# Hybrid encoder step on one core: half A's convolution schedule, the order of high and low products, and the first two FFN tiles of half B reordered

## The chip, the cores and the metric

The kernel runs on 1 core of one Trainium2 chip. Its five engines run their own instruction streams and meet at semaphores: TensorE (PE, matmuls, with weight loads as PEld), VectorE (DVE), ScalarE (ACT), GpSimd (POOL) and SyncE (SP, which issues the DMAs of the weights). The metric is the device time of one execution in microseconds (us), lower is better. It is a median of several runs.

## The reference

A two-layer encoder on 1,024 prompt frames and 32 sample frames, all in float32. Layer 0 is a convolution module and a SwiGLU FFN; layer 1 is windowed attention with 16 query and 4 key heads, and a second FFN.

```
for i in range(DEPTH):
    hp, hs = rms_norm(xp, g_mix[i]), rms_norm(xs, g_mix[i])
    if i % N_MIXERS == 0:
        u = h @ w_pw1 + b_pw1;  g = a * sigmoid(gate)        # 1024 -> 2 x 1024
        c = depthwise causal conv of g, width 31, + b_dw      # per channel
        m = silu(layer_norm(c, ln_g, ln_b)) @ w_pw2 + b_pw2
    else:
        q, k, v = qkv_proj(h, w_qkv, qn_g, kn_g)              # RMS norm per head
        m = sink_attention(q, k, v, dist, valid, sinks) @ w_o
    xp, xs = xp + mp, xs + ms
    x = x + (silu(h @ w_gate) * (h @ w_up)) @ w_down          # h = rms_norm(x, g_ffn[i])
```

The first output is the 1,056 frames after both layers; the others are the last 30 convolution inputs and the newest keys and values.

## The kernel before

**Data.** Channels lie on the 128 partitions, so the width of 1,024 is 8 channel tiles, k = 0 to 7. The frames are cut in half A (512 frames) and half B (544: 512 prompt frames and the 32 sample frames, written as two column groups of 272). The residual `x` stays in SBUF.

**High and low parts.** Each float32 operand is split: a high part (rounded to fp32r) and a low part (the rest). A weight tile of 128 output channels is loaded to `raw`, ScalarE makes `whi` (function `hi`), GpSimd makes `wlo` (`lo`); there are two of each. An activation has `hi_[h]` and `lo_[h]` (`hAh`, `hAl`, `hBh`, `hBl`). One output tile (`proj`) is three groups of products: `whi` times high and low part, alternating over k (L346), then `wlo` times high part (L355). A `mid` hook issues other work between the two. The FFN's down projection (`down`, L560 and L567) does the same with the activations `act`.

**Norms.** A norm is named by its event `ev`: mix0A, mix0B, lnA, ffn0A, lnB, mix1A, ffn0B, mix1B, ffn1A, ffn1B. ScalarE squares 8 tiles, they are summed (for lnA and ffn0A by TensorE itself, `square_sum`, L381, eight matmuls; otherwise by GpSimd, `sum_squares`, L1919), TensorE takes the mean over channels with a matrix of ones (`norm_mean`), ScalarE makes the factor (`factor`: Ln, then Exp), VectorE scales (`x_norm`, L1401), ScalarE rounds the high part (`n_hi_part`, or `ln_part` with Silu for the convolution's norm), VectorE subtracts for the low part (`low`, L1406). The scaled tile lies in one of two buffers `nrm`, so tile k waits for the low part of tile k - 2.

**Order of the work.** All of it is written out by hand, engine by engine. `SEQ1` lists the 29 tiles of the first projection: gate ("g") and value ("a") tiles of half A for channels 0 to 2, then A and B alternating, then three more of B. Within it the convolution of half A runs: of 31 taps per channel tile, `NP["A"]` = 10 are done by ScalarE (product, L987) and GpSimd (sum in `accp`, L1940), and 21 by VectorE in two PSUM banks X and Y (L1508), followed by two joins (X with the GpSimd sum, L1515; then Y, L1520). GpSimd adds the tiles to `csum`; TensorE takes the mean (`("lm", "A")`), VectorE centres, squares follow, the norm lnA, then eight tiles `p2` of the second projection. The convolution of half B runs under the p2 tiles and FFN 0 of half A. Then: p2 of B, QKV of A, FFN 0 of B with the attention of A under it, and so on; the last stretch is FFN 1 of A, then FFN 1 of B (11 groups G, each of four tiles gate/up and, from G = 1 on, the down projection of G - 1).

**PSUM.** Eight banks in two rings of four: `take(key, h, ring)` gives the next bank (two, on an even number, for half B) and waits until its former user has been read. Products use ring 0; small things, and the convolution, ring 1.

**Waits of note.** `act_low` (L1604) makes the low part of the FFN's activations and stands, on VectorE, between the additions `add_to_x` (L1592) of down tiles 3 and 4. In the QKV part of half B, `head_mean` number 2 is issued in the middle of tile 5 and takes two banks of ring 1.

## Time and profile before

| | us |
|---|---|
| median of 3 runs | 2289.23 (2288.8 to 2289.9) |
| profiled execution, its own time | 2286.99 |
| its span, first to last instruction | 2285.2 |
| TensorE busy | 2228.7 |
| VectorE, ScalarE, GpSimd busy | 1111.8, 1037.8, 1113.6 |
| mean granted clock of TensorE | 0.988 of full speed |

The profiled execution's own time is 1.8 us above its span. Engine rows are sums over the span; an engine that is idle costs time only where TensorE waits for it.

### The profile page before, as it was taken

What the parts mean: (1) busy time and instruction counts of PE and PEld (TensorE: products, weight loads), DVE (VectorE), ACT (ScalarE), POOL (GpSimd) and SP (SyncE); (2) the same over time, 40 slices, a digit from 0 to 9 for tenths busy, and PEclk for the clock granted to TensorE, in tenths of its full rate; (3) what the DMA queues carried; (4) which work ended last, traced back from release to release, by engine and by line L of the source; (5) the groups of instructions that cost most, each with busy time, mean ns of one, the idle gap of its engine ahead of it and who ended that gap; (6) DMA issues with size and microseconds to landing.
All of it is one profiled execution on the core that took longest, in us unless ns stands there. A gap on an engine that the chain in (4) does not pass through costs nothing.

```text
span 2285.2 us, 34556 instructions
## 1 busy us (share of the span) xinstructions
PE 2228.7 (98%) x13954; PEld 2017.0 (88%) x13954; DVE 1111.8 (49%) x1822; ACT 1037.8 (45%) x1659; POOL 1113.6 (49%) x573
## 2 busy tenths in 40 slices
PE   8998899999999999999999999999999999999999
PEld 7797678887889799999999898888888989999999
DVE  4987668873434544445443535454554142222223
ACT  6544655533524654544552466465655332222222
POOL 3787569975446533333334544333333443443433
PEclk9999899999999999999999999999999999999999
DMA  4111123332333522222222342222222323233222
GB/s 149 47 54 57 57 65 102 97 102 83 94 100 89 104 86 79 75 74 75 75 75 84 93 99 84 83 83 78 80 84 75 92 77 99 93 102 93 84 89 90
DMA packets 313644, 194.15 MB, mean 85 GB/s; under 512 B 40374, under 2 KB 286734, under 8 KB 313486
## 3 DMA queue, kind: packets, MB, share of 16 engines
q1 hardware_dynamic: 311608, 190.83, 28.3%
q8 instruction: 112, 1.84, 0.3%
q10 hardware_dynamic: 1878, 1.11, 0.2%
q14 instruction: 46, 0.38, 0.1%
HBM read 184.39 MB, written 5.10 MB: 83 GB/s over the span
## 4 chain that ended last, share of the span: by engine, by line
PE 91%; POOL 3%; DVE 2%; ACT 2%; issue 1%; DMA 0%; ACTq 0%; DVEq 0%; POOLq 0%
PE ps L346 42%; PE ps L355 21%; PE ps L560 14%; PE ps L567 7%; PE ps L530 2%; POOL accp L1940 2%; PE ps L516 1%; PE ps L364 1%; PE ps L492 1%; PE ps L491 1%; POOL wlo L1909 1%; PE ps L381 1%; DVE x L1592 1%; POOL rs L1919 0%; DVE sq L1401 0%
## 5 line engine op out<-in xcount | busy, mean ns | idle before, releaser
L1909 POOL TENSOR_TENSOR wlo<-raw,whi 128x1024 fp32r<-128x1024 f32 x342 | 838.9, 2453 | 1095.4 <-PE ps L355 763.7
L857 ACT ACTIVATE whi<-raw 128x1024 fp32r<-128x1024 f32 x342 | 361.8, 1058 | 628.4 <-PE ps L346 366.6
L346 PE MATMUL ps<-hBh,whi 128*128 128x272 f32 x2112 | 440.7, 290 | 6.0 <-DVE x L1592 3.2
L346 PE MATMUL ps<-hBl,whi 128*128 128x272 f32 x2112 | 440.0, 290 | 0.0
L346 PE MATMUL ps<-hAh,whi 128*128 128x512 f32 x1056 | 418.7, 397 | 18.5 <-DVE hAl L1406 10.5
L346 PE MATMUL ps<-hAl,whi 128*128 128x512 f32 x1056 | 416.1, 394 | 0.0
L1592 DVE TENSOR_TENSOR x<-ps,x 128x512 f32<-128x512 f32 (+1 forms) x368 | 258.4, 705 | 244.2 <-PE ps L567 181.3
L346 PEld LDWEIGHTS ps<-hBh,whi 128*128 128x128 f32 x2112 | 334.2, 190 | 8.9 <-issue 4.9
L346 PEld LDWEIGHTS ps<-hBl,whi 128*128 128x128 f32 x2112 | 332.4, 189 | 0.0
L355 PE MATMUL ps<-hBh,wlo 128*128 128x272 f32 x2112 | 291.2, 290 | 0.0
L355 PEld LDWEIGHTS ps<-hBh,wlo 128*128 128x128 f32 x2112 | 273.7, 188 | 2.5 <-issue 1.9
L355 PE MATMUL ps<-hAh,wlo 128*128 128x512 f32 x1056 | 270.6, 399 | 2.9 <-POOL wlo L1909 2.9
L346 PEld LDWEIGHTS ps<-hAh,whi 128*128 128x128 f32 x1056 | 200.3, 190 | 68.8 <-DVE hAl L1406 11.1
L1599 DVE TENSOR_TENSOR s<-ps,s 128x512 f32<-128x512 f32 (+1 forms) x88 | 62.3, 708 | 369.3 <-PE ps L355 367.2
L355 PEld LDWEIGHTS ps<-hAh,wlo 128*128 128x128 f32 x1056 | 197.0, 190 | 46.6 <-issue 4.3
L346 PEld LDWEIGHTS ps<-hAl,whi 128*128 128x128 f32 x1056 | 200.9, 190 | 40.8
L1940 POOL TENSOR_TENSOR accp<-accp,prod 128x512 f32<-128x512 f32 (+1 forms) x144 | 199.7, 1387 | 25.2 <-ACT prod L987 12.4
L1665 DVE TENSOR_TENSOR ptl<-ps,pth 128x512 fp32r<-128x512 f32 (+1 forms) x64 | 42.1, 658 | 167.1 <-ACT pth L1088 167.1
L1508 DVE SCALAR_TENSOR_TENSOR ps<-gxB,dwc,ps 128x574 f32<-128x574 f32 x152 | 114.1, 811 | 0.0
L1088 ACT ACTIVATE pth<-ps 128x512 fp32r<-128x512 f32 (+1 forms) x64 | 36.6, 572 | 167.6 <-PE ps L516 167.6
L1508 DVE SCALAR_TENSOR_TENSOR ps<-gxA,dwc,ps 128x512 f32<-128x512 f32 x152 | 101.8, 749 | 0.0
L560 PE MATMUL ps<-act0h,whi 128*128 128x272 f32 (+1 forms) x288 | 78.6, 327 | 4.5 <-DVE x L1592 3.9
(254 smaller groups left out, 3161.7 us busy)
## 6 DMA issues: line engine op xcount, KB each, us to landing
raw<-in_w_gate_dram SPq DMA_DIRECT2D x88, 512.0 KB, 3.8
raw<-in_w_up_dram SPq DMA_DIRECT2D x88, 512.0 KB, 3.8
raw<-in_w_down_dram SPq DMA_DIRECT2D x88, 512.0 KB, 3.6
raw<-in_w_pw_dram SPq DMA_DIRECT2D x38, 512.0 KB, 4.0
raw<-in_w_qkv_dram SPq DMA_DIRECT2D x32, 256.0 KB, 3.7
raw<-in_w_o_dram SPq DMA_DIRECT2D x64, 128.0 KB, 2.9
stage<-in_x_prompt_dram SPq DMA_DIRECT2D x8, 512.0 KB, 5.7
raw<-in_w_qkv_dram SPq DMA_DIRECT2D x8, 512.0 KB, 3.7
```

The lines of the kernel that those rows point to most:

```text
L346: ins = nc.tensor.matmul(o, whi[n % 2][:, P * k:P * (k + 1)], src[:, k, c0:c0 + w], start=(k == 0 and src is hi_[h]), stop=False)
L355: ins = nc.tensor.matmul(o, wlo[n % 2][:, P * k:P * (k + 1)], hi_[h][:, k, c0:c0 + w], start=False, stop=(k == KD - 1))
L530: ins = nc.tensor.matmul(ps[0:HD, 6, 0:256], v[:, slot, HD * g:HD * (g + 1)], p[:, 256 * z:256 * (z + 1)], start=(z == 0 and w == 0), stop ...
L560: ins = nc.tensor.matmul(o, whi[n % 2][:, wc], src[s + e][:, c0:c0 + w], start=(e == 0 and src is ach), stop=False)
L567: ins = nc.tensor.matmul(o, wlo[n % 2][:, wc], ach[s + e][:, c0:c0 + w], start=False, stop=(e == 1))
L857: nc.scalar.activation(whi[n % 2][:], raw[n % 2][:], ACT.Copy).then_inc(w_hi, 1)
L1508: link(nc.vector.scalar_tensor_tensor((X, Y)[q % 2], two(gx[h][:, c, t:t + w]), dwc[:, KD * t + c:KD * t + c + 1], (X, Y)[q % 2], ALU.mult ...
L1592: nc.vector.tensor_tensor(xd, pt(key), xd, ALU.add).then_inc(fr(key), 1)
L1599: nc.vector.tensor_tensor(s, pt(key), s, ALU.mult).then_inc(fr(key), 1)
L1665: nc.vector.tensor_tensor(ptl[:, 0:w], ps[:, 5, 0:w], f(pth[:, 0:w]), ALU.subtract).then_inc(pt_lo, 1)
L1909: nc.gpsimd.tensor_tensor(wlo[n % 2][:], raw[n % 2][:], f(whi[n % 2][:]), ALU.subtract).then_inc(w_lo, 1)
L1940: nc.gpsimd.tensor_tensor(accp[p % 2][:, 0:w], accp[p % 2][:, 0:w], prod[r % 2][:, 0:w], ALU.add).then_inc(padd, 1)
```

## The change

- The convolution of half A gives ScalarE and GpSimd 9 taps instead of 10, VectorE 22 instead of 21. X and Y alternate between banks 4, 5 and 6, 7, and the two joins of a channel tile stand behind the first six taps of the next. VectorE starts it at once with 8 and 10 steps (before 6 and 6), then 8 per slot (7).
- `SEQ1` loses two tiles of B. Between the mean of the convolution and the p2 tiles now stand one tile ahead of the squares' sum and two behind it; the two value tiles B 1 and B 2 come after p2.
- The squares of lnA are added in pairs by GpSimd (four matmuls instead of eight); those of ffn0A by VectorE (`sum_of_squares`; two matmuls).
- The scaled tiles have eight buffers (`full_`, in the place of the low part) instead of two. The first tile that uses new activations (`new`) does all high products, then `wlo`, then all low ones. `whi` of such a tile is free at its end.
- The first gate and up tiles of the last FFN of half B are done together (`proj_pair`): high products of both, low ones last.
- At the start: 10 and 14 matmuls with no use for their result (`keep_busy`), parameters in another order, the products of tile 0 between the matmuls that scale half A, diagonals of half B by ScalarE, activation tables loaded ahead. The x groups of frames 512 on use a ring of two banks.
- The norm means of mix1A, ffn0B and ffn1A go to ring 1; that of mix1B one tile later, that of ffn1B one half of a down projection earlier. `act_low` stands behind all eight additions. GpSimd's two sums in FFN 0 A, G = 6, stand behind the next `wlo`. In QKV of B the low part of the sample values moves ahead of the head norm of slot 6.

```diff
-NP = {"A": 10, "B": 10}
+NP = {"A": 9, "B": 10}
...
-SEQ1 += [("g", "B", 0), ("a", "B", 0), ("g", "B", 1)]
+SEQ1 += [("g", "B", 0)]
...
+    for p in range(KD):
+        out += own[p][:6] + ends + own[p][6:-2]
+        ends = own[p][-2:]
+    return out + ends
...
-        want = 0 if s < 2 else 1 if s in (5, 6) else 6 if s < 5 else 7
+        want = (0, 0, 8, 10, 10, 2, 2)[s] if s < 7 else 8
...
+def products_a(s):
+
+    return 0 if s < 2 else 2 * s - 1 if s < 7 else 11 + (KD * NP["A"] - 11) * (s - 6) // (len(SEQ1) - 7)
...
+        RINGS = [(0, 4), (4, 4), (6, 2)]
...
+                new = ev and (ev, h) != ("mix0", "A") and waited.get(h, 0) < h_need(ev, KD - 1)
...
+                    ins = product(whi, hi_, k, start=(k == 0))
+                    if not new:
+                        ins = product(whi, lo_, k)
...
+                for k in range(KD):
+                    ins = product(wlo, hi_, k, stop=(not new and k == KD - 1))
+                if new:
+                    for k in range(KD):
+                        wait_h(h, ev, k)
+                        ins = product(whi, lo_, k, stop=(k == KD - 1))
...
+            keep_busy(10)
...
+            keep_busy(14)
+            half_a(0)
+            half_a(1)
...
+                     ahead=(lambda k: half_a(k + 2)) if s == 0 else None)
...
-            pe.wait_ge(csummed, KD - 1)
-            mean(("lm", "A"), "A", ones_d, csum)
-            proj("B", ("a", "B", 1), "mix0", load(("a", 1)))
-            square_mean("lnA", lambda k: pe.wait_ge(sq_ready, k + 1))
+            b = take(("lm", "A"), "A")
+            pe.wait_ge(csummed, KD - 2)
+            nc.tensor.matmul(ps[:, b, :], ones_d[:], csum[:, 0:512], start=True, stop=False)
+            pe.wait_ge(c_ready, KD)
+            nc.tensor.matmul(ps[:, b, :], ones_d[:], gx["A"][:, ORDER["A"][-1], 0:512], start=False, stop=True
+                             ).then_inc(pfull[b], 1)
+            proj("B", ("a", "B", 0), "mix0", load(("a", 0)))
+            take(("mean", "lnA"), "A")
+            square_sum("lnA", range(0, KD, 2), lambda i: pe.wait_ge(sq_pairs, i + 1))
+            for c in (1, 2):
+                proj("B", ("g", "B", c), "mix0", load(("g", c)))
...
-                        norm_mean(ev)
+                        norm_mean(ev, 1)
...
-                if n >= 2:
-                    act.wait_ge(whi_free, n - 1)
+                if n - 2 in whi_read:
+                    act.wait_ge(whi_free, whi_read[n - 2])
+                elif n >= 2:
+                    full(act, last_tile[n - 2])
...
                 for k in range(k0, k1):
                     x_norm(ev, k, gain)
-                    if k % 2:
-                        low(ev[-1], ev[:-1], k - 1)
-                        low(ev[-1], ev[:-1], k)
+                for k in range(k0, k1):
+                    low(ev[-1], ev[:-1], k)
...
+                nc.vector.tensor_tensor(sqx[:, 0, :], sqx[:, 0, :], sqx[:, k, :], ALU.add).then_inc(sq_sums, 1)
...
-                        if d == 3:
+                        if d == (3 if G in (0, NG - 1) else KD - 1):
                             act_low(l, h, G, 1)
...
+            lo()
+            for i in range(KD // 2):
+                pool.wait_ge(sq_ready, 2 * i + 2)
+                nc.gpsimd.tensor_tensor(sqx[:, 2 * i, :], sqx[:, 2 * i, :], sqx[:, 2 * i + 1, :], ALU.add
+                                        ).then_inc(sq_pairs, 1)
+            lo()
             lo()
```

`proj_pair`, new, called for the first two tiles of FFN 1 of half B:

```
for n, out in zip(ns, outs_of):
    pe.wait_ge(w_hi, n + 1)
    for k in range(KD):
        pe.wait_ge(h_hi[h], h_need(ev, k))
        ...                                # whi x high part
    pe.wait_ge(w_lo, n + 1)
    ...                                    # wlo x high part
for key, n, out in zip(keys, ns, outs_of):
    for k in range(KD):
        wait_h(h, ev, k)
        ...                                # whi x low part
```

What stands on VectorE around one join of half A's convolution (gxA is its input and result, dwc the taps, accp the GpSimd sum, dv the semaphore of VectorE's own chain, padd that of GpSimd's additions). Before:

```order
L1508 SCALAR_TENSOR_TENSOR ps<-gxA,dwc,ps 128x512 [waits dv] x12
L1469 SCALAR_TENSOR_TENSOR gxA<-ps,col,s 128x512 [waits pfull3,pfree2]
L1508 SCALAR_TENSOR_TENSOR ps<-gxA,dwc,ps 128x512 [waits dv] x7
L1515 SCALAR_TENSOR_TENSOR accp<-ps,col,accp 128x512 [waits dv,padd]
L1520 TENSOR_TENSOR gxA<-ps,accp 128x512 [waits dv]
L1504 TENSOR_SCALAR ps<-gxA,dwc 128x512 [waits gx_edges,pfree1]
```

And in the change:

```order
L1647 SCALAR_TENSOR_TENSOR ps<-gxA,dwc,ps 128x512 [waits dv] x6
L1643 TENSOR_SCALAR ps<-gxA,dwc 128x512 [waits c_ready,gx_edges,pfree1]
L1643 TENSOR_SCALAR ps<-gxA,dwc 128x512
L1647 SCALAR_TENSOR_TENSOR ps<-gxA,dwc,ps 128x512 [waits dv] x4
L1654 SCALAR_TENSOR_TENSOR accp<-ps,col,accp 128x512 [waits dv,padd]
L1659 TENSOR_TENSOR gxA<-ps,accp 128x512 [waits dv]
```

The wait for GpSimd's sum (padd) moved behind six taps of the next tile.

On TensorE, around the mean of the convolution of half A. Before:

```order
L355 MATMUL ps<-hBh,wlo 128x272 x15
L364 MATMUL ps<-csum,ones_d 128x512 [waits pfree2,csummed]
L346 MATMUL ps<-hBh,whi 128x272 [waits w_hi,pfree0]
...
L381 MATMUL ps<-sqx,ones_d 128x512 [waits sq_ready,pfree2]
L381 MATMUL ps<-sqx,ones_d 128x512 [waits sq_ready] x7
```

And in the change, up to the first p2 tile:

```order
L559 MATMUL ps<-csum,ones_d 128x512 [waits csummed,pfree2]
L561 MATMUL ps<-gxA,ones_d 128x512 [waits c_ready]
L395 MATMUL ps<-hBh,whi 128x272 [waits w_hi,pfree0]
...
L469 MATMUL ps<-sqx,ones_d 128x512 [waits sq_pairs,pfree2]
L469 MATMUL ps<-sqx,ones_d 128x512 [waits sq_pairs] x3
...
L395 MATMUL ps<-hAh,whi 128x512 [waits h_hiA,w_hi,pfree6]
L395 MATMUL ps<-hAh,whi 128x512 [waits h_hiA] x7
L395 MATMUL ps<-hAh,wlo 128x512 [waits w_lo]
L395 MATMUL ps<-hAh,wlo 128x512 x7
L395 MATMUL ps<-hAl,whi 128x512 [waits h_readyA] x8
```

The mean has two tiles of B less ahead of it, the sum of squares is four matmuls, two tiles of B (left out in the second gap) follow it, and the first p2 tile asks for its low parts last.

On TensorE in QKV of half B, from the middle of tile 4 to the middle of tile 5. Before (rs is the sum of squares of the norm ffn1A, tq the squared heads):

```order
L364 MATMUL ps<-rs,ones_d 128x512 [waits pfree0,ssum]
...
L364 MATMUL ps<-tq,ones_h 128x272 [waits pfree7,pfree6,hsq]
```

And on TensorE and then VectorE in the change (the last row but one is the sample values' low part, which frees their bank, 7):

```order
L780 MATMUL ps<-ident,qraw 32x128 [waits pfree6]
L780 MATMUL ps<-ident,qraw 32x128
L456 MATMUL ps<-rs,ones_d 128x512 [waits pfree4,ssum]
...
L456 MATMUL ps<-tq,ones_h 128x272 [waits pfree7,pfree6,hsq]
```

```order
L1539 SCALAR_TENSOR_TENSOR hA<-x,col,rs 128x512 [waits rs_ready]
L1539 SCALAR_TENSOR_TENSOR hA<-x,col,rs 128x512
L1544 TENSOR_TENSOR hAl<-hA,hAh 128x512 [waits h_hiA] x2
L1881 TENSOR_TENSOR vtl<-ps,vth 32x256 [waits kv_hi]
L1841 SCALAR_TENSOR_TENSOR qraw<-qraw,col,tq 128x544 [waits hrs]
```

The mean moved from bank 0 (ring 0) to bank 4 (ring 1); the ring's next pair is therefore 6 and 7, where the second value tile and the sample values lie, and bank 7 is freed only behind the two low parts.

## Rows read from the trace of the kernel before

**Rows 1.** The page, part 1: engine busy time, share of the span, instructions.

```profile
PE 2228.7 (98%) x13954; PEld 2017.0 (88%) x13954; DVE 1111.8 (49%) x1822; ACT 1037.8 (45%) x1659; POOL 1113.6 (49%) x573
```

**Rows 2.** Waits of TensorE: total us, times, longest us.

```profile
PE ps L346 <- DVE hAl L1406: 10.5, 6, 7.1
PE ps L364 <- POOL csum L1962: 8.9, 1, 8.9
PE ps L346 <- ACT s L968: 4.8, 1, 4.8
...
PE ps L346 <- DVE x L1592: 4.0, 2, 3.2
PE ps L560 <- DVE x L1592: 3.9, 3, 1.3
PE ps L346 <- ACT qraw L1143: 3.7, 2, 1.9
...
PE ps L355 <- POOL wlo L1909: 2.9, 1, 2.9
...
PE ps L364 <- POOL rs L1919: 1.1, 1, 1.1
```

**Rows 3.** Windows: length; busy PE, PEld, DVE, ACT, POOL; PEclk, DMA share, GB/s.

```profile
60.40:72.20 11.80, 6.97 (x24) 5.66 (x25) 7.74 (x12) 7.63 (x11) 5.91 (x4) 0.86 0.31 89
...
83.10:193.50 110.40, 110.40 (x725) 102.71 (x724) 99.16 (x157) 56.53 (x79) 97.30 (x70) 1.00 0.16 45
193.50:216.30 22.80, 13.92 (x98) 12.67 (x98) 17.65 (x28) 9.20 (x13) 21.43 (x15) 0.82 0.22 64
216.30:237.30 21.00, 13.89 (x65) 9.74 (x64) 8.05 (x15) 11.94 (x17) 2.46 (x2) 0.91 0.17 51
237.30:288.70 51.40, 50.13 (x194) 37.90 (x195) 39.12 (x57) 33.08 (x45) 36.48 (x22) 0.88 0.22 62
288.70:318.80 30.10, 27.35 (x138) 20.32 (x137) 16.95 (x25) 14.65 (x19) 8.98 (x6) 0.94 0.18 52
...
536.00:550.00 14.00, 11.12 (x44) 8.71 (x43) 3.31 (x6) 6.11 (x9) 11.63 (x7) 0.88 0.26 75
...
1856.30:1880.50 24.20, 20.98 (x102) 18.30 (x101) 18.57 (x25) 12.47 (x16) 7.14 (x3) 0.86 0.21 60
```

**Rows 4.** The chain in order of time: start us, us, what.

```profile
223.32 6.88 PE ps L381 x16
...
1797.15 4.02 PE ps L346 x32
1803.16 4.03 PE ps L346 x32
```

**Rows 5.** Timeline, TensorE, the last third of two half A tiles.

```profile
98.84 1.98 PE L355 MATMUL ps<-hAh,wlo 128*128 128x512 f32 x8
...
104.28 1.98 PE L355 MATMUL ps<-hAh,wlo 128*128 128x512 f32 x8
```

**Rows 6.** Timeline, VectorE, half A convolution: a run of taps, the last join.

```profile
86.64 9.31 DVE L1508 SCALAR_TENSOR_TENSOR ps<-gxA,dwc,ps 128x512 f32<-128x512 f32 x14
...
212.24 0.69 DVE L1520 TENSOR_TENSOR gxA<-ps,accp 128x512 f32<-128x512 f32 x1
```

**Rows 7.** Timeline, ScalarE: a table load and the last high part of the norm.

```profile
230.21 1.28 ACT L881 ACT_TABLE_LOAD   x1 [7.38 <-PE ps L381]
...
245.67 0.63 ACT L906 ACTIVATE hAh<-sq 128x512 fp32r<-128x512 f32 x1
```

**Rows 8.** Timeline, VectorE, `act_low`, beside a GpSimd pass and alone.

```profile
956.50 2.85 DVE L1604 TENSOR_TENSOR act3l<-s,act3h 128x544 fp32r<-128x544 f32 x1
...
1851.54 0.68 DVE L1604 TENSOR_TENSOR act1l<-s,act1h 128x512 fp32r<-128x512 f32 x1
```

**Rows 9.** Timeline, half B QKV, tile 5: ScalarE, then VectorE.

```profile
1353.30 1.06 ACT L857 ACTIVATE whi<-raw 128x1024 fp32r<-128x1024 f32 x1 [3.31 <-PE ps L346]
...
1354.91 1.29 DVE L1406 TENSOR_TENSOR hAl<-sq,hAh 128x512 fp32r<-128x512 f32 x2 [3.37 <-ACT hAh L893]
```

More of the change, by code:

```diff
@@ L971, in _, with taps @@
             done = {"A": 0, "B": 0}
-            def taps(h, j):
-                for i in range(done[h], products(h, j)):
+            def taps(h, n):
+                for i in range(done[h], n):
                     p, c, t, r = in_order(h, i)
```

375 lines of the change are left out of this document (230 added, 145 removed).

## The prediction

> **What bounds the kernel now.** I read the page's first part, then the waits of TensorE, then windows around each long wait. TensorE is busy 98% of the span [rows 1], so a gain can only come from its waits, from stretches at the lower clock, or from matmuls left out. A half B tile starts every 6.03 us [rows 4], a half A tile every 5.44 us [rows 5]; neither changes. The eight kinds of wait in [rows 2] sum to 39.8 us. Most lie before 320 us. There TensorE waits for ScalarE's sigmoid (4.8 us, once), for the last GpSimd sum of half A's convolution (8.9 us, once) and for low parts (10.5 us in six waits). Then the clock: PEclk is a share of 2.4 GHz and is a mean of two levels, so 0.86 over 11.8 us means that 3.3 us ran at 1.2 GHz, which costs 1.65 us. In each window of [rows 3] with a PEclk below 1, TensorE had waited for some us shortly before. By the windows, (1 - PEclk) times length is 1.7, 4.1, 1.9, 6.2, 1.8 and 1.7 us for the first row and the third to the seventh, and 3.4 us for the last.
>
> **The sum, part by part.** Positions are those of the profiled execution, whose own time of 2286.99 us is 2.2 us under the median; I subtract gains from the median.
>
> (a) To 83.1 us: 7. At the start VectorE's diagonals no longer stand behind the copy of parameters, but 14 matmuls and the interleaved scaling do fill TensorE; by the rates of the other matmuls the first tile should end some 3.3 us earlier. The next tile takes the same bank and so waits for a sigmoid, 1 us. Two x groups of five tiles run through two banks instead of four: each may stall 0.9 us, -1.8. Diagonals of half B from ScalarE, +1.3. The wait for a sigmoid (4.8 us [rows 2]) was long because ScalarE stood behind products that GpSimd had not taken; with two products a slot instead of three and the table loaded ahead, only the sigmoid, 1 us, is left: +3.8. The clock stays up: +1.7 [rows 3]. Sum 7.3.
>
> (b) The mean of the convolution: 3. A tap costs VectorE 9.31 / 14 = 0.665 us [rows 6]. From 37.6 us on (my estimate: half A's first value was scaled by 41 us before, less some 3.3) it has 192 steps, 128 us; value products, 10 us; 16 passes for half B's norm, 12 us; waits for sigmoid and factors, 2 us. That is 190. In the norm passes both inputs are in SBUF; [rows 8] shows such a pass at 2.85 us beside a GpSimd pass and 0.68 alone. GpSimd has some 10 us of work in that stretch; I take 4 us of collisions, bounds 0 and 8. The convolution ends at 194 instead of 212.9 [rows 6], the mean at 195. Before it was there at 216.3, but with two more tiles (12.1 us) done. So 216.3 - 195 - 12.1 - 1 (a clock that may fall in a wait of 4 us) = 8.2, of which 7.3 were had in (a): +1 to +5 over the bounds, 2.5 taken. Hidden under this is the join: it may now come 4 us later than its sum without a stall.
>
> (c) From the mean to the first p2 tile: 11.6. Before 237.3 - 216.3 = 21.0 [rows 3]. Now one tile, 6, until the last pair sum 3.5 with four matmuls (6.88 us for eight before [rows 4]) and two tiles, 12.1: 21.6, of which 12.1 are the moved tiles.
>
> (d) Eight p2 tiles: 2.2. Before 51.4 us [rows 3], of which 43.5 are work. The high parts of the norm ended 16.1 us after the mean of squares (230.2 [rows 4] to 246.3 [rows 7]). The two tiles cover 12.1. Two table loads of 1.28 [rows 7] leave the chain (-2.6), two `hi` of 1.06 [rows 9] enter it (+2.1), and, at a guess, one collision of a scaling or low pass (+1.7, bounds 0 and 4.4, two at the 2.2 of [rows 8]): 17.3. TensorE gets the last high part 5.2 us into the p2 tile, which after it still has 3.6 us of products instead of ending at 5.44: a stall of 3.6, and 2 for the clock. 43.5 + 5.7 = 49.2.
>
> (e) To the second FFN tile: 7.6. Before 30.1 us [rows 3]. Two matmuls instead of eight save 5.1. The norm ffn0A takes Ln, Exp, 8 scalings and 8 low parts, some 13.3 us and up to 4.6 of collisions, over 8.1 of cover and 5.2 until the last low part is needed: stall 0 to 4.6, taken 2.3, against some 5 before. VectorE's six extra sums (0.6 us, or 2 us in a collision) may cost 0 to 3, taken 0.5.
>
> (f) `wlo` late at 543 us: 2.9 [rows 2] and 1.7 for the clock [rows 3]: 4.5, since GpSimd's two sums no longer stand ahead of it.
>
> (g) The norm mean in QKV of A: 1.9 of the 3.7 us for qraw [rows 2], and 1.2 for the clock that fell there too: 3.
>
> (h) `act_low` behind the additions: the three waits of L560 (3.9 us [rows 2]) go, and two short ones in FFN 0 of A (1): 4.9. It stalled the additions because it took 2.85 us [rows 8]. Behind them it has over 5 us until `down` needs it.
>
> (i) Means of mix1A and mix1B: 1.1 and 1.9, from L1919 (1.1) and the 0.8 of L1592 [rows 2]: 3.
>
> (j) QKV of B: -3. The mean in ring 1 saves 1.8 us of waiting for qraw. But `head_mean` 2 now takes banks 6 and 7, and 7 is freed by the sample values' low part, which stands on VectorE behind two low parts of the norm; these wait for two high parts, those for a `hi` that waits for the high products of this very tile 5. Read from the trace: the `hi` starts at 1353.30, right after the products, the two low passes end at 1356.2, the pass behind them takes 0.4 [rows 9]. So a new wait of 3.5 us in the middle of tile 5, perhaps with 1.2 for the clock.
>
> (k) FFN 1 of half B: 5. The window 1856.3 to 1880.5 has TensorE idle for 3.2 us (24.20 less 20.98) and 3.4 of clock [rows 3]; part of the low clock fell on the idle time itself, so I take 6.1 for both. Now the mean is taken 5 us earlier and only the fourth bank's addition is missing at the start: 0.8 us. 6.1 - 0.8 = 5.3.
>
> Sum: 7.3 + 2.5 + 11.6 + 2.2 + 7.6 + 4.5 + 3 + 4.9 + 3 - 3 + 5.3 = 48.9, so 2289.2 - 49 = 2240 us.
>
> **A rule against it.** [Rows 8] shows a VectorE pass that starts during a GpSimd pass and ends 0.6 us after it. The Trainium skill (SBUF — State Buffer, Who interferes with whom) says that a VectorE instruction with two SBUF inputs and a GpSimd instruction that reads SBUF exclude each other, and whichever comes second is fully blocked. The trace agrees, and by that rule VectorE's new sums over squares and the earlier norm passes, under a GpSimd that is hardly ever idle, are the worst case; it is the second rival.
>
> **Rivals.**
> 1. The convolution does not end sooner. In 83.1 to 193.5 VectorE is busy 99 of 110 us and GpSimd 97 [rows 3]; VectorE gets a tap more per tile. If it ended at 212.9 as before, the mean would come at 214 and (b) be 216.3 - 214 - 12.1 - 7.3 = -17 instead of 2.5: 2260. Against it: it starts 7 us sooner, and loses the waits at the joins. 8%.
> 2. The passes with two SBUF inputs collide. 54 of them (16 for mix0B, 16 for lnA, 6 sums, 16 for ffn0A) now run beside GpSimd work. Each collision costs up to 2.2 us [rows 8]. Ten more on the path than I count: 2262. 10%.
> 3. Slower. The same mechanism, at the same place, if VectorE lost every race: 54 x 2.2 = 119 us. It decides from 25 more collisions on the path (55 us), 2295. Against it: GpSimd has seven passes or so in each of these stretches, and a pass can be lost to only one of them. 2%.
> 4. All waits before 320 us vanish, since the lower bounds of collisions hold and the clock stays up: (b) +2.5, (d) +5.5, (e) +3: 2229, and without the new wait in (j) 2225. 12%.
> 5. The stalls only move: no change. 1%.
>
> **How the numbers follow.** The forecast has the rest, 67%, and its own range is 2230 to 2254: the bounds of (a) +-3, (b) -2 to +3, (d) and (e) -7 to +4, (g) to (k) +-3, not all at once. To hold 8 in 10 I take half of rivals 1 and 2 and of 4: 2227 to 2258. Within 0.2% (4.6 us) is about what a measurement of this kernel can't tell from no change. Faster 0.97 (forecast and rivals 1, 2, 4), same 0.01, slower 0.02.
>
> **What the profile after would show.** (a) Value tile A 2 starts near 59 us. (b) The last join ends at 190 to 196 us and TensorE's wait for it is about 4 us. (c, d) The p2 tiles start near 217 us with one wait of 3 to 5 us for high parts. (f, h) No wait for `wlo` L1909 and none of the down products for additions. (j) A new wait of 3 to 4 us for VectorE at `head_mean` in QKV of B. (k) At most 1 us ahead of the paired tiles. The forecast is wrong if VectorE ends the convolution after 200 us, or if half B's tiles in that stretch begin to wait for their banks, since the value products stand behind VectorE's steps: then (b) goes first.

## The result and the profile after

| | before | after |
|---|---|---|
| median (runs) | 2289.02 us (4) | 2258.39 us (4: 2257.91 to 2258.83) |
| span of the profiled execution | 2285.2 us | 2257.0 us |
| TensorE busy | 2228.7 us | 2214.2 us |
| mean granted clock | 0.988 | 0.995 |

The ratio is 0.9867, with a 95% interval of 0.985 to 0.9884. The change makes the kernel 30.6 us faster. The forecast was 2240 us, 49 us faster, with a range that ended at 2258, just under the result: about three fifths of the forecast gain came. (One execution of an experiment below, that with GpSimd's part a slot earlier, took 2713 us at a mean clock of 0.752; it is left out of that kernel's median.) The engines' rows of the page ([rows 1] has those of before):

```profile
PE 2214.2 (98%) x13984; PEld 2013.2 (89%) x13984; DVE 1113.2 (49%) x1831; ACT 1035.6 (46%) x1659; POOL 1120.6 (50%) x568
```

TensorE is still busy in 98% of the span. TensorE's waits, as in [rows 2] (total us, times, longest us):

```profile
PE ps L395 <- DVE gxB L1612: 7.5, 1, 7.5
PE ps L561 <- DVE gxA L1659: 6.2, 1, 6.2
PE ps L437 <- ACT hBh L1019: 4.0, 1, 4.0
PE ps L456 <- DVE vtl L1881: 3.5, 1, 3.5
PE ps L395 <- ACT hAh L1030: 2.7, 2, 1.8
...
PE ps L395 <- DVE gxA L1606: 2.2, 1, 2.2
...
PE ps L609 <- DVE col L1770: 1.5, 1, 1.5
```

Of the waits in [rows 2] those for `wlo`, for additions ahead of down products (L560 there) and for the norm sum `rs` are gone. The wait for low parts in six pieces (10.5 us) is gone too, but for one of 0.6 us at the start, and in its place stands one of 7.5 us for the scaling of a value tile of half B (L1612). A new one of 4.0 us is for a high part of the last norm (L437, in `proj_pair`), one of 3.5 us for `vtl` (L1881). The wait for the convolution is 6.2 us instead of 8.9.

Windows of the profile after; the columns are those of [rows 3]:

```profile
191.10:199.40 8.30, 2.13 (x6) 0.78 (x5) 4.97 (x8) 2.99 (x4) 7.23 (x5) 0.73 0.22 64
199.40:222.40 23.00, 23.00 (x155) 20.57 (x154) 13.62 (x22) 17.61 (x25) 9.91 (x6) 0.95 0.17 49
222.40:271.20 48.80, 45.98 (x194) 37.09 (x193) 39.88 (x53) 30.57 (x41) 38.06 (x21) 0.97 0.29 86
271.20:300.70 29.50, 21.63 (x126) 18.77 (x125) 24.40 (x36) 12.24 (x18) 14.33 (x9) 0.88 0.25 72
1839.30:1858.60 19.30, 14.08 (x98) 13.50 (x97) 9.20 (x15) 5.98 (x8) 8.46 (x3) 0.91 0.20 55
```

The second to fourth rows answer to the rows at 216.3, 237.3 and 288.7 of [rows 3], the last one to that at 1856.3. The worst is the fourth: 29.5 us of which TensorE works 21.6, at a mean PEclk of 0.88.

**Where the gain went.** The table compares the start of the same matmuls in the two traces. "Ahead by" is the start before less the start after. At the mean of the convolution the two tiles moved behind it (12.06 us) are taken off. "Step" is the change from the row above.

| point | before | after | ahead by | step | forecast |
|---|---|---|---|---|---|
| `wlo` products of value tile A 2 (a) | 70.43 | 63.97 | 6.5 | +6.5 | +7.3 |
| tile behind the mean of the convolution (b) | 215.24 | 199.41 | 3.8 | -2.7 | +2.5 |
| first p2 tile (c) | 237.30 | 222.37 | 14.9 | +11.2 | +11.6 |
| tile behind the last p2 tile (d) | 288.54 | 271.22 | 17.3 | +2.4 | +2.2 |
| `wlo` products, FFN 0 A, tile 2 (e) | 322.28 | 304.31 | 18.0 | +0.7 | +7.6 |
| `wlo` products, behind the late `wlo` (f) | 550.22 | 527.99 | 22.2 | +4.3 | +4.5 |
| a tile behind the mean of mix1A (i) | 708.83 | 685.45 | 23.4 | +1.2 | +1.1 of 3 |
| QKV A behind the mean (g) | 773.76 | 746.60 | 27.2 | +3.8 | +3 |
| FFN 0 B behind the third `act_low` (h) | 1139.92 | 1108.20 | 31.7 | +4.6 | +4.9 |
| behind the mean of mix1B (i) | 1300.13 | 1266.31 | 33.8 | +2.1 | +1.9 of 3 |
| QKV B and first FFN tiles (j) | 1430.85 | 1402.09 | 28.8 | -5.1 | -3 |
| third tile of the last FFN (k) | 1890.56 | 1862.70 | 27.9 | -0.9 | +5.3 |

(a), (c), (d), (f), (g), (h) and (i) came within 1 us of their forecast. They are read from the two traces alone: no experiment takes one of them out by itself, apart from the order of products and the matmuls at the start. (b), (e), (j) and (k) did not, and together they are 20 of the 21 us that the profiled execution lacks. The experiments go to these four places, and to the order of products that the title of the change names.

### The profile page after: what moved, and what is told of

The parts are those of the page before. It is cut to its first block, busy times and chain, and to the rows that moved or that the text cites. A ratio compares the mean times of both kernels' runs of the same rounds, so it can differ in the third digit from the quotient of the medians.

```text
span 2257.0 us, 34608 instructions
## 1 busy us (share of the span) xinstructions
PE 2214.2 (98%) x13984; PEld 2013.2 (89%) x13984; DVE 1113.2 (49%) x1831; ACT 1035.6 (46%) x1659; POOL 1120.6 (50%) x568
## 4 chain that ended last, share of the span: by engine, by line
PE 90%; DVE 3%; POOL 3%; issue 2%; ACT 1%; DMA 0%; SPq 0%; DVEq 0%; POOLq 0%; ACTq 0%
PE ps L395 60%; PE ps L680 15%; PE ps L687 7%; POOL accp L2089 2%; PE ps L648 2%; PE ps L634 1%; PE ps L456 1%; DVE hB L1539 1%; PE ps L609 1%; PE ps L610 1%; POOL wlo L2058 1%; POOL rs L2068 0%; PE ps L497 0%; DVE hA L1539 0%; DVE hAl L1544 0%
## 5 line engine op out<-in xcount | busy, mean ns | idle before, releaser
L2058 POOL TENSOR_TENSOR wlo<-raw,whi 128x1024 fp32r<-128x1024 f32 x342 | 849.8, 2485 | 1057.0 <-PE ps L395 658.3
L395 PE MATMUL ps<-hBh,whi 128*128 128x272 f32 x2080 | 428.4, 289 | 5.0 <-DVE gxA L1606 2.2
L395 PE MATMUL ps<-hBl,whi 128*128 128x272 f32 x2080 | 427.6, 289 | 0.0
L395 PE MATMUL ps<-hAh,whi 128*128 128x512 f32 x1056 | 411.7, 394 | 12.7 <-DVE gxB L1612 7.5
L395 PE MATMUL ps<-hAl,whi 128*128 128x512 f32 x1056 | 409.1, 392 | 0.0
L395 PEld LDWEIGHTS ps<-hBh,whi 128*128 128x128 f32 x2080 | 325.4, 189 | 8.2 <-issue 3.5
L395 PEld LDWEIGHTS ps<-hBl,whi 128*128 128x128 f32 x2080 | 324.0, 188 | 0.0
L2089 POOL TENSOR_TENSOR accp<-accp,prod 128x574 f32<-128x574 f32 (+1 forms) x136 | 191.6, 1409 | 30.8 <-ACT prod L1111 19.1
L1647 DVE SCALAR_TENSOR_TENSOR ps<-gxA,dwc,ps 128x512 f32<-128x512 f32 x160 | 107.3, 746 | 0.0
```

Source lines behind the costliest of these rows:

```text
L395: ins = nc.tensor.matmul(o, wt[n % 2][:, P * k:P * (k + 1)], src[h][:, k, c0:c0 + w], start=start, stop=stop)
L1647: link(nc.vector.scalar_tensor_tensor((X, Y)[q % 2], two(gx[h][:, c, t:t + w]), dwc[:, KD * t + c:KD * t + c + 1], (X, Y)[q % 2], ALU.mult ...
L2058: nc.gpsimd.tensor_tensor(wlo[n % 2][:], raw[n % 2][:], f(whi[n % 2][:]), ALU.subtract).then_inc(w_lo, 1)
L2089: nc.gpsimd.tensor_tensor(accp[p % 2][:, 0:w], accp[p % 2][:, 0:w], prod[r % 2][:, 0:w], ALU.add).then_inc(padd, 1)
```

## The experiments

Each kernel is the changed kernel with the edit shown, unless the text names another; the kernel before, timed beside them, had medians between 2288.7 and 2289.6 us. I compare medians with the 2258.4 us of the changed kernel. A stretch at the low clock is 3.4, 6.8 or 10.2 us long in the traces of the experiments and costs half of that. Traces of kernels that are the same up to that place differ by one or two of them, so a difference of 2 us needs its local reading in the trace as well. In the diffs "..." and comments stand for code that is left out. Line numbers in an experiment's rows are its own, a few off those of the change.

### (e) The value tiles' reader behind the norm

Timeline of the changed kernel, VectorE and TensorE around the first FFN tile (start us, us, what, idle before and its releaser):

```profile
279.98 7.45 DVE L1539 SCALAR_TENSOR_TENSOR hA<-x,col,rs 128x512 f32<-128x512 f32 x8 [5.04 <-ACT rs L1009]
...
287.36 4.89 DVE L1544 TENSOR_TENSOR hAl<-hA,hAh 128x512 fp32r<-128x512 f32 x8
...
292.18 1.96 DVE L1612 SCALAR_TENSOR_TENSOR gxB<-ps,col,s 128x272 f32<-128x272 f32 x6
...
293.25 2.08 PE L395 MATMUL ps<-hAh,whi 128*128 128x512 f32 x4 [7.51 <-DVE gxB L1612]
```

TensorE ends the value tile B 2 at 285.7 us and then stands until 293.25. It doesn't wait for the norm: it waits for `gxB` (L1612), the scaling that frees the banks of the value tile B 1. The two value tiles fill all four banks of ring 0, and their scaling (the function `glu`) stands behind all 16 passes of the norm ffn0A.

```diff
-            norm_parts("ffn0A", C_FFN[0], 0, KD)
             glu("B", 1)
+            for k in range(KD):
+                x_norm("ffn0A", k, C_FFN[0])
             glu("B", 2)
+            for k in range(KD):
+                low("A", "ffn0", k)
```

> VectorE scales value tile B 1 ahead of the norm ffn0A and value tile B 2 between its eight scalings and its eight low parts; nothing else differs from the changed kernel (2258.4 us). Theory: the first gate tile of FFN 0 waits 7.5 us at 285.7 us only for the bank that value tile B 1 holds, because its reader stands behind 16 norm passes; the wait goes or falls to the 1 to 2 us that the high and low parts need, and the low clock after it (6.8 us at half speed) with it: 6 to 9 us faster, 2249 to 2252. Rival: the norm itself is late, as the forecast had it, and the bank only hides that wait: the tile then waits for high parts for 5 us or more, and the time falls by less than 2 us, 2257.

2253.1 us, 5.3 us faster than the change: the theory, though short of the 6 to 9 us that it expected. Its trace:

```profile
285.11 1.09 PE L395 MATMUL ps<-hAh,whi 128*128 128x512 f32 x4
...
286.53 2.06 PE L395 MATMUL ps<-hAh,whi 128*128 128x512 f32 x4 [0.33 <-ACT hAh L1019]
...
288.00 4.87 POOL L2155 COPY stc<-gxB 128x90 f32<-128x90 f32 x1 [6.20 <-DVE gxB L1612]
...
323.06 0.50 PE L395 MATMUL ps<-hAh,whi 128*128 128x512 f32 x1 [1.59 <-ACT s L1191]
```

The first FFN tile starts at 285.1, straight behind the tile ahead of it, and waits 0.33 us for a high part. Its `wlo` products start 8.4 us sooner than in the changed kernel (296.82 against 288.43). So the bank was the cause; the rival has fallen. At the second tile, the point (e) of the table, this kernel is 7.5 us ahead of the changed one: with the bank free (e) would read +8.2, where the forecast had +7.6. At 355 us 5.2 of the 8.4 are left, and at 389 us 4.3: at 323.06 TensorE waits 1.6 us for a sigmoid that stands on ScalarE behind products that GpSimd has not taken. I put that down to GpSimd's copy at 288.00: GpSimd stood idle for 6.2 us ahead of it, and it took 4.87 us beside VectorE's low parts (0.26 us in the changed kernel, where they are done by then).

> The kernel with the value tiles' scaling ahead (2253.1 us), in which GpSimd's copy of half B's first rows (4.87 us there, idle before it for 6.2 us) no longer stands ahead of the first low part and sums of FFN 0 but behind those of its second tile. Theory: of the 8.1 us won at the first FFN tile 3.8 were given back because GpSimd, idle and then blocked at that copy, ran late with its sums, ScalarE behind it with products and a sigmoid (1.6 us of waiting at 321 us, 1.1 at 374); with the copy out of the way they are kept: 2249.5 to 2251. Rival: the tiles of FFN 0 are paced by the convolution of half B as a whole, wherever GpSimd starts: 2253 within 0.8.

```diff
-            freed(pool, ("a", "B", 2))             # and the copy, ahead of FFN 0
+                            if (G, b) == (0, 1):
+                                first_rows()       # the same, behind the sums of tile 2
```

This edit is made in the kernel of 2253.1 us. It takes 2259.0 us, 5.9 slower: both theories missed. Its waits of TensorE:

```profile
PE ps L395 <- ACT hAh L1019: 2.1, 2, 1.7
...
PE ps L395 <- DVE hAl L1544: 1.5, 2, 1.3
```

GpSimd's `wlo` now falls on the norm's passes instead. TensorE waits for a high part (L1019, 1.7 us) and a low part (1.3 us) of ffn0A, and the `wlo` products of the second tile start 4.5 us later. By 380 us all but 1.3 of these 4.5 us have come back. The rest of the 5.9 us goes with the clock: the three unprofiled runs have a mean of 0.993 to 0.994, those of the kernel it starts from 0.996 to 0.997. No trace shows where it fell, since the profiled execution was the fastest of the four (2255.7 us). That the copy caused what was given back stays unproven.

### (b) What ends the convolution

Timeline of the changed kernel: the first join of half A's convolution that has to wait, and the last one, with GpSimd's sums:

```profile
68.29 3.74 POOL L2089 TENSOR_TENSOR accp<-accp,prod 128x512 f32<-128x512 f32 x2 [3.36 <-ACT prod L1111]
...
72.07 0.75 DVE L1654 SCALAR_TENSOR_TENSOR accp<-ps,col,accp 128x512 f32<-128x512 f32 x1 [2.62 <-POOL accp L2089]
...
194.08 2.67 POOL L2089 TENSOR_TENSOR accp<-accp,prod 128x512 f32<-128x512 f32 x2 [0.44 <-POOL accp L2089]
...
196.79 0.75 DVE L1654 SCALAR_TENSOR_TENSOR accp<-ps,col,accp 128x512 f32<-128x512 f32 x1 [2.17 <-POOL accp L2089]
197.57 0.69 DVE L1659 TENSOR_TENSOR gxA<-ps,accp 128x512 f32<-128x512 f32 x1
```

VectorE waits 2.6 us at the first join and 2.2 at the last for GpSimd's sum; the last join ends at 198.26 us. The forecast had 194, and had called this wait hidden. At the last join the sum stands on GpSimd behind a `wlo` (188.34 to 190.76 us). The first is late for another reason: GpSimd had been idle for 3.36 us, waiting for ScalarE's product. That product stood behind four high parts of the norm mix0B, and they waited for scalings, one of which took 2.84 us instead of 0.69 beside a `wlo`. At the six joins between, VectorE does not wait.

The two waits, 4.8 us, are the whole delay. The forecast's other terms, read from VectorE's timeline: the steps start at 39.3 us (37.6 forecast), 192 steps take 127.6 us (128), the value products 10.1 (10), the 16 norm passes 14.0 with their collisions (16), waits for sigmoid and factors 2.3 (2).

```diff
-NP = {"A": 9, "B": 10}
+NP = {"A": 10, "B": 10}
```

> The changed kernel with ten taps of half A's convolution on ScalarE and GpSimd instead of nine, as the kernel before has them; VectorE has 184 steps instead of 192, the slots of the first joins are shifted to fit. Theory that VectorE's steps set the end of the convolution: 8 x 0.665 = 5.3 us sooner, of which the mean gains 4 to 5: 2254. Theory that GpSimd sets it (97.6 us of work in the 115 us before the end, eight more sums of 1.3 us): the end comes 3 to 10 us later: 2262 to 2268. Both bind in turn: 2258.4 within 2.

(The slots of the first joins are shifted to fit.) 2265.9 us, 7.5 slower, inside the range of the second theory. VectorE has 5.3 us less to do, and yet its last join comes 5.0 us later. It waits for GpSimd's sum at five of the eight joins, 11.0 us in all, and longest at the last:

```profile
201.80 0.75 DVE L1654 SCALAR_TENSOR_TENSOR accp<-ps,col,accp 128x512 f32<-128x512 f32 x1 [4.25 <-POOL accp L2089]
```

The same with eight products (every second slot has nine of VectorE's steps instead of eight):

```diff
-NP = {"A": 9, "B": 10}
+NP = {"A": 8, "B": 10}
```

> The changed kernel with eight taps of half A's convolution on ScalarE and GpSimd instead of nine; VectorE has 200 steps instead of 192. With ten taps the mean came 5.0 us later. Theory that GpSimd alone sets the end: 5 us sooner, 2253.5. Theory that both engines bind, and nine is the balance: VectorE's eight more steps cost 5.3 us and save at most the 4.8 us that it waits at the first and the last join: 2258 to 2260, the wait for the last join's GpSimd sum gone. Rival: 2256, if the last slot's wait goes and collisions become fewer.

2263.3 us, 4.9 slower, and outside what any of its theories gave. Only the first join still waits (0.5 us), and yet the last one starts 1.0 us later than in the changed kernel:

```profile
197.78 0.75 DVE L1654 SCALAR_TENSOR_TENSOR accp<-ps,col,accp 128x512 f32<-128x512 f32 x1
```

So with ten products GpSimd sets the end of the convolution, with eight VectorE, and nine is where both bind. The profiled execution with eight is as long as the changed kernel's (2257.1 against 2257.0 us of span) and was the fastest of four; what made the other three 4 us longer no trace shows, beyond a mean clock of 0.993 instead of 0.994. By its trace eight products cost 1.0 us at the join and nothing at the end; that they cost 4.9 us stands on the three other runs. Spreading GpSimd's part so that it ends a slot earlier does not help:

```diff
-    ... 11 + (KD * NP["A"] - 11) * (s - 6) // (len(SEQ1) - 7)
+    n = ... 11 + (KD * NP["A"] - 11) * (s - 6) // (len(SEQ1) - 8)
+    return min(n, (KD - (s < len(SEQ1) - 3)) * NP["A"])
```

> The products and sums of half A's convolution on ScalarE and GpSimd are spread so that they end one slot earlier (68 of 72 are due where 65 were, and all of them one slot ahead of the last). Theory: at the end of the convolution VectorE waits 2.2 us for GpSimd's sum of the last channel tile, which stands behind a low part of a weight tile; without that wait the mean comes 2.2 us sooner: 2256.2. Rival: VectorE, not GpSimd, sets the end, through its 192 steps and its norm passes, and the two more collisions that a fuller GpSimd makes eat the rest: 2258.4 within 0.7.

2259.2 us (2254.3, 2259.2 and 2259.3): near the rival's time, but not for its reason. Its waits at the mean:

```profile
PE ps L560 <- POOL csum L2112: 2.5, 1, 2.5
...
PE ps L562 <- DVE gxA L1660: 1.4, 1, 1.4
```

The join's wait for GpSimd is gone, the join ends 1.5 us sooner, and now the sum over channels (`csum`), also on GpSimd, is late. Of the 1.5 us the tile behind the mean keeps 0.3. The work of GpSimd was only put in another order.

### (k) The pair of the last FFN

Timeline of the changed kernel, VectorE's scalings (L1539) between the additions, GpSimd's `wlo`, and the pair's first product:

```profile
1830.64 2.24 DVE L1539 SCALAR_TENSOR_TENSOR hB<-x,col,rs 128x544 f32<-128x544 f32 x1
...
1837.19 2.40 POOL L2058 TENSOR_TENSOR wlo<-raw,whi 128x1024 fp32r<-128x1024 f32 x1 [4.89 <-ACT whi L981]
...
1837.29 2.88 DVE L1539 SCALAR_TENSOR_TENSOR hB<-x,col,rs 128x544 f32<-128x544 f32 x1
...
1842.79 0.66 ACT L1019 ACTIVATE hBh<-hB 128x544 fp32r<-128x544 f32 x1 [0.64 <-DVE hB L1539]
...
1843.75 2.61 PE L437 MATMUL ps<-hBh,whi 128*128 128x272 f32 x10 [4.04 <-ACT hBh L1019]
```

A scaling alone takes 0.77 us. The second of the eight took 2.24, and the sixth 2.88, beside the `wlo` of 1837.19 (each is a single pass: the expectations below miscount them). The eighth high part is ready at 1843.4 and TensorE, done with the down tiles at 1839.6, waits 4.0 us for it. A low stretch follows (3.4 us from 1843.5 on, 1.7 us lost). Then the third tile waits for the bank of the pair's gate tile, whose sigmoid stands behind a table load:

```profile
1856.59 1.28 ACT L1191 ACT_TABLE_LOAD   x1
...
1858.61 0.49 PE L395 MATMUL ps<-hBh,whi 128*128 128x272 f32 x2 [1.19 <-ACT s L1191]
```

The kernel before has no such wait. There a whole tile of 6 us lies between the end of the gate tile and the next use of its banks; in the pair only the 2.2 us of the other tile's low products do (until 1857.4 us), and `whi`, table and sigmoid take ScalarE until 1858.5. The three terms are 6.9 us, where the forecast had 0.8. No kernel here was built without the pair, so that the third is due to it is read from the rows and not tested.

```diff
+                if n == len(tags) - 1 - tags[::-1].index(("G", 1, 0)):
+                    pool.wait_ge(xn_ready, 7 * KD)
```

> The changed kernel in which GpSimd makes the low part of the first paired weight tile (at 1837.2 us) only after VectorE's last scaling of the norm ffn1B; it is needed 3.6 us after that. Theory: of the 4.0 us that TensorE waits for the last high part, 2.1 are this one collision (2.88 us for two passes and more, 0.77 alone) and 1.5 the one before it (2.24); without the second the wait is 1.9 to 2.2 and the clock stays up or not: 1.9 to 3.6 us faster, 2254.8 to 2256.5. Rival: additions and scalings take turns at the pace of TensorE's own down tiles, and the last high part comes late whatever GpSimd does: 2258.4 within 0.7, the wait still 3.5 or more.

2255.3 us, 3.1 faster. The sixth and eighth scaling, the `wlo`, and the same wait:

```profile
1837.14 0.77 DVE L1539 SCALAR_TENSOR_TENSOR hB<-x,col,rs 128x544 f32<-128x544 f32 x1
...
1839.73 0.77 DVE L1539 SCALAR_TENSOR_TENSOR hB<-x,col,rs 128x544 f32<-128x544 f32 x1
...
1840.67 5.23 POOL L2060 TENSOR_TENSOR wlo<-raw,whi 128x1024 fp32r<-128x1024 f32 x2 [8.51 <-DVE hB L1539]
...
1841.46 2.24 PE L437 MATMUL ps<-hBh,whi 128*128 128x272 f32 x16 [1.89 <-ACT hBh L1019]
```

The wait is 1.9 us, the low clock behind it is gone too, and the pair's `wlo` products start 3.7 us sooner: the theory. One collision, moved away, gives 3 us. The `wlo` could be moved because it was early: it ended at 1839.6 us in the changed kernel, and its first product starts at 1847.3. The other way to give it slack:

```diff
-                    if (l, h) == (1, "A"):
-                        x_norm("ffn1B", d, C_FFN[1])
+                    if (l, h) == (1, "A") and d < 4:
+                        x_norm("ffn1B", 2 * d, C_FFN[1])
+                        x_norm("ffn1B", 2 * d + 1, C_FFN[1])
```

> In the last down projection of FFN 1 of half A VectorE does two scalings of the norm ffn1B ahead of each of the additions 0 to 3 instead of one ahead of each of 0 to 7. Theory: the wait of 4.0 us for the last high part ahead of the paired tiles comes from two scalings that collide with GpSimd's low parts of the weights (2.24 for two and 2.88 for two passes and more, where 0.77 is the price of one alone), at the end of a chain without slack; early scalings have slack, so the wait falls under 1 us and the clock stays up: 3 to 5 us faster, 2253.5 to 2255.5. Rival: the additions come later now, and TensorE waits for their banks what it no longer waits for high parts: 2258 (within 1).

2257.3 us, 1.1 faster, with runs from 2256.9 to 2259.4 us: the rival. The wait for the high part is gone from the list, and TensorE waits for the additions instead, ahead of two down products (and 1.1 us ahead of the pair):

```profile
PE ps L680 <- DVE x L1738: 2.2, 2, 1.9
```

The two collisions (3.62 us for the first two scalings, 3.00 for the last two) are still there and now delay the additions. VectorE is late by what the collisions cost, and the order only chooses who waits.

### (j) The sample values' low part

Timeline of the changed kernel, QKV of half B (the norm's factor is there at 1313.6 us):

```profile
1315.93 1.41 DVE L1539 SCALAR_TENSOR_TENSOR hA<-x,col,rs 128x512 f32<-128x512 f32 x2
...
1319.05 1.29 DVE L1544 TENSOR_TENSOR hAl<-hA,hAh 128x512 fp32r<-128x512 f32 x2 [1.71 <-ACT hAh L1019]
1320.26 0.41 DVE L1881 TENSOR_TENSOR vtl<-ps,vth 32x256 fp32r<-32x256 f32 x1
...
1320.81 1.73 PE L456 MATMUL ps<-tq,ones_h 128*128 128x272 f32 x4 [3.47 <-DVE vtl L1881]
```

The chain is the one that the forecast had: two scalings, two low parts that wait for high parts behind a `hi`, then L1881, then TensorE after 3.47 us, then 3.4 us at the low clock, 1.7 us lost: 5.2 us, where the forecast had 4.7.

```diff
                         value_low(h, 1)
+                        if h == "B":               # moved from slot 6, behind norm_parts
+                            dve.wait_ge(kv_hi, 11)
+                            nc.vector.tensor_tensor(vtl[0:TS, 6, :], ...)
```

> In QKV of half B the sample values' low part stands ahead of the norm's two scalings and two low parts of slot 5 on VectorE, instead of behind them. Theory: it alone frees bank 7, for which TensorE waits 3.5 us in the middle of tile 5; the wait goes and so does the low clock after it (3.4 us at half speed, 1.7 us lost): 4.5 to 5.2 us faster, 2253.2 to 2254. Rival: the ring of the mean is the matter, and the next user of ring 1 waits instead: under 1.5 us faster.

2254.1 us, 4.3 faster: the theory, 0.2 us short of its range. The low part comes before the scalings, and TensorE's wait is no longer in its list:

```profile
1314.77 0.40 DVE L1899 TENSOR_TENSOR vtl<-ps,vth 32x256 fp32r<-32x256 f32 x1
1315.10 1.39 DVE L1539 SCALAR_TENSOR_TENSOR hA<-x,col,rs 128x512 f32<-128x512 f32 x2
```

The `wlo` products of tile 5 start 5.2 us sooner, of which 1.0 us was already there ahead of this place, and those of the next tile 6.5, since the low stretch is gone too. The other 1.8 us that (j) lost lie in the first FFN tiles: TensorE waits 1.5 us for `col` (L609 in the waits above), because two short VectorE passes (`qsl`, 0.2 us alone, and a copy of 2 columns, 0.16 alone) took 2.38 and 2.35 us beside `wlo` passes there. Before the change only `qsl` met one at this place (1.78 us), and TensorE did not wait.

### The order inside a tile, and the start

```diff
-                new = ev and (ev, h) != ("mix0", "A") and waited.get(h, 0) < h_need(ev, KD - 1)
+                new = False
```

> The changed kernel in which every tile alternates products of high and low parts, as before the change; only the first two tiles of the last FFN keep their own order. Theory of the forecast: the new order hides up to 3.6 us of products behind the norm in the first p2 tile and about 1 us each in the first tiles of the QKV, FFN and mix0 stages: 3 to 7 us slower, 2261.5 to 2265. Rival: the waits after this change are for banks, high parts and GpSimd and not for low parts, so the order inside the tile is worth little: 2258.4 within 1.5.

2257.1 us, 1.3 faster than the change, which is within the spread of its runs (2256.3 to 2259.1): the rival, and a miss for the forecast. TensorE waits for low parts again, 2.5 us of it at the first p2 tile, where the changed kernel waits 2.7 us in two pieces for high parts (L1030 in its waits above):

```profile
PE ps L395 <- DVE hAl L1544: 3.1, 2, 2.5
```

At the p2 tile the low parts follow the high ones closely (the last low part ends at 229.1 us in the changed kernel, and the last high product starts at 227.5), so there is little for the order to hide. By the start of the tiles that follow, the new order is worth nothing at the p2 tile and in the QKV stages, and 0.8 us at the first FFN tile. The trace of the old order is 2.6 us ahead at the end for two other reasons: it has no low stretch at 1321 us, behind the wait for `vtl` (1.6), and no wait for `col` near 1400 us (1.8). The same `vtl` wait stands in both traces, and I did not look into why the stretch is missing.

```diff
-            keep_busy(10)
-            keep_busy(14)
```

> The changed kernel without the 24 matmuls at the start whose result is not used. Theory of the forecast: they keep the clock at its high level; without them TensorE starts at the low one for some 7 us, as before the change at 13.7 us, and loses 2 to 3.4 us: 2260.5 to 2262. Rival: TensorE waits for the transfers of x and for ScalarE's squares at the start anyway, so that the loss is hidden or made up by the end of the convolution: 2258.4 within 0.7.

2261.9 us (2258.2 to 2262.8), 3.5 slower: the theory in time, but the trace does not show its cause. TensorE waits for the transfer of x and for `diag` at the start, but the first tile's `wlo` products start 1.3 us sooner than in the changed kernel, the second half B tile's are 0.3 later, and no low stretch lies in the first 20 us. Instead the clock is low at 86 to 92 us, and longer behind the first p2 tile (PEclk 0.76 from 226 to 240 us, 0.88 in the changed kernel). By TensorE's last `wlo` products this trace is 1.5 us behind; the other 1.2 us by which it is longer lie behind TensorE's work, in the output. And both low stretches stand just so in traces of kernels that do have the 24 matmuls (the 87 us one in four of them, the long one behind the first p2 tile in three, the one with early scalings among both). So the runs show the kernel slower without these matmuls; that they keep the clock up is not shown.

```profile
PE ps L489 <- DMA stage<-in_x_prompt_dram: 4.5, 1, 4.5
...
PE ps L506 <- DVE diag L1568: 2.3, 1, 2.3
```

Two windows of the same kernel:

```profile
86.00:92.00 6.00, 6.00 (x38) 6.00 (x37) 6.00 (x10) 4.37 (x7) 5.86 (x4) 0.72 0.00 1
226.00:240.00 14.00, 12.57 (x43) 10.12 (x44) 6.00 (x8) 8.00 (x12) 6.52 (x4) 0.76 0.17 49
```

### Together

> The changed kernel with three edits at once: value tiles scaled ahead of and between the norm ffn0A (alone 5.3 us faster), the sample values' low part ahead of the norm parts (alone 4.3 us faster), and the low part of the first paired weight tile after the last scaling (unknown, 0 to 3.6). Theory that the places are independent: 2258.4 - 5.3 - 4.3 - 2 = 2247, 2245 to 2249. Rival: a gain that is made early is given back at a later wait, as 3.8 us of the first one were: 2250 or more.

The edits of (e), (j) and (k, the moved `wlo`) at once. 2248.2 us, runs of 2245.0 to 2249.6; ratio to the kernel before 0.982 (0.9805 to 0.9834). This is inside the range of the first theory, and the trace is 9.4 us ahead behind the pair. Alone the three gave 5.3, 4.3 and 3.1 us, 12.7 in sum, and together they give 10.2; with runs that spread over 4.6 us the runs do not tell whether some was given back. The sigmoid's wait behind the first FFN tiles is there, as in the kernel with (e) alone:

```profile
PE ps L395 <- ACT s L1191: 2.8, 2, 1.6
```

> The combined kernel (2248.2 us, runs of 2245.0 to 2249.6) with the old order inside a tile: products of high and low parts alternate in all tiles but the paired ones. In the changed kernel the old order was not slower (2257.1 against 2258.4), but there the first FFN tile stood for its bank until high and low parts were all there. Theory: with the bank free the order pays there, since the low parts end some 6 us behind the first high product: the 2 us of wlo products no longer lie behind the last low part, 1.5 to 3 us slower, 2249.7 to 2251.2. Rival: the order is worth nothing anywhere: 2248.2 within 0.8, or up to 1.5 us faster as before.

Both theories missed: 2244.3 us (2243.8 to 2244.8, five runs), the fastest kernel here, 44 us under the kernel before (ratio 0.9804, 0.979 to 0.9818).

```profile
PE ps L395 <- DVE hAl L1544: 6.5, 3, 3.4
PE ps L561 <- DVE gxA L1659: 5.0, 1, 5.0
```

Locally the theory held at one tile: the waits for low parts rise to 6.5 us in three pieces, 3.4 of them at the first FFN tile, whose successor starts 1.0 us later than in the combined kernel where it had been 1.6 sooner: the old order loses 2.6 us here, 1.7 of it by a low stretch at 289.2 us. Then it comes back. With the first tile later, the sigmoid's wait of 1.6 us is not there, and by 378 us this kernel is 2.0 us ahead; the `col` wait at 1394 is not there either (+1.9), and one stretch at the low clock less behind the p2 tile and ahead of the pair (1.6 and 1.0). So the new order gains at its tile and nothing at the end; that the others took it back is what the rows show, that it would be so in every run is not shown.

## Why the prediction was wrong

**Right.** TensorE's waits were the place to look, and the method (waits, then the clock behind them) gave (a), (c), (d), (f), (g), (h) and (i) within 1 us each. The wait in (j) was forecast at 3.5 us and is 3.5.

**The order of products.** The forecast took it for granted in (c) to (e). Two kernels without it are no slower: 1.3 us faster, within the spread, and 3.9 us faster. At its own tiles it gains 0.8 and 2.6 us, at the first FFN tile alone. What the change gained came from its other parts.

**(e), 7 us.** The step that failed is "13.3 us and up to 4.6 of collisions, over 8.1 of cover ... stall 0 to 4.6". It counted when the low parts would be there and forgot where the tile would be put. The term of banks was missing: two value tiles of half B hold all four of ring 0 until VectorE has scaled them, and `glu` stands behind the norm. The prediction's last sentence named this mechanism, but for the stretch before the mean, where the one such wait of half B's tiles (2.2 us at 86.9 us, L1606) was covered by the wait at the mean. Moving the scaling gave 8.4 us at the place and 5.3 at the end.

**(b), 5 us.** "Hidden under this is the join: it may now come 4 us later than its sum without a stall" is the step. The reading was of VectorE alone, 192 steps from 37.6 us on. GpSimd, with 97 of 110 us busy in [rows 3], bound nearly as much; its sum was late by 2.6 and 2.2 us at two joins, 4.8 us where the forecast had nothing. The trace of before had the sign: there VectorE waits for the sum at four of eight joins (L1515), 5.4 us in all. Nine products are the balance of the two, as the runs with ten and eight show. A slip in the sum adds to it: 216.3 - 195 - 12.1 - 1 is 8.2, so that (b) is 8.2 - 7.3 = 0.9 with the 4 us of collisions taken, and -3 to +5 over their bounds, not 2.5 and +1 to +5. 8.2 less the 4.3 us by which the convolution ended late is 3.9, and the table has 3.8. The first rival is not what happened: the convolution ended 14.7 us sooner (212.93 against 198.26), not at the same time.

**(k), 6 us.** "Only the fourth bank's addition is missing at the start: 0.8 us" left out the high parts and the pair's own banks: the wait was 4.0 us, with 1.7 of clock and 1.2 of waiting for a sigmoid behind the pair. The mean had been pulled ahead, but scalings and additions still take turns, so that the last scaling comes with the last addition, and two scalings in that chain collided with `wlo` for 1.5 and 2.1 us. This is the second rival's mechanism, at a place where I had not looked for it. Taking one of the two away gave 3.1 us.

**(j), 2 us.** The term was under-sized: the new wait and its clock are 5.2, of which the ring returned 1.9, and a second pair of collisions in the first FFN tiles, which I had not looked for, cost 1.8 more.

**Collisions.** They did not cost more than the forecast carried where it looked for them: 3.4 us over the 16 passes of mix0B, where it took 4, and 1.9 us over the scalings of ffn0A, where it took 2.3. They cost 3.6 us at (k) and 1.8 at (j), where it had none. The trace shows them in both directions: a VectorE scaling of 0.77 us takes 2.2 to 2.9 beside `wlo`, and a GpSimd copy of 0.26 us took 4.87 under VectorE's low parts. The Trainium skill (SBUF — State Buffer, Who interferes with whom) has it that the side that comes second is fully blocked. The trace agrees: the sixth scaling of ffn1B, begun at 1837.29 us, ends 0.6 us behind the `wlo` that was there first.

**Smaller slips.** The stall in (d) is 5.2 + 3.6 - 5.44 = 3.4 by its own terms, and a half B tile takes 6.01 us by [rows 4]. Neither moves the result.

## What to carry to other kernels

When a tile is moved, follow its bank as well as its data: who reads it last, what stands ahead of that reader on its engine, and how many banks the ring has left. When work is split between two engines that meet at a join, sum both sides and not only the one that looks busy; the balance is found by a step to either side. A late VectorE pass with both inputs in SBUF that ends a chain should have no GpSimd pass beside it: delaying one `wlo` that had been ready 7.7 us ahead of its first product gave 3 us. When two tiles are done as a pair, ask what the third one waits for.
